# A fused two-block network on one core: the two opening slabs of each output projection worked in step, and seven eighths of one pair moved into a recurrence's last head

## The reference

```python
def gdn_mixer(h, w_in, conv_w, a_log, dt_bias, norm_g, w_out):
    ...
    o = chunk_gated_delta_rule(to_bhtd(q), to_bhtd(k), to_bhtd(v),
                               jnp.transpose(g, (0, 2, 1)), jnp.transpose(beta, (0, 2, 1)))
    o = jnp.transpose(o, (0, 2, 1, 3)).astype(h.dtype)
    o = rmsnorm(o, norm_g) * jax.nn.silu(gate.reshape(B, T, GDN_HEADS, GDN_HEAD_DIM))
    return o.reshape(B, T, GDN_VALUE_DIM) @ w_out

def swiglu(h, w_gate, w_up, w_down):
    return (jax.nn.silu(h @ w_gate) * (h @ w_up)) @ w_down

x = x + gate_m * y
x = x + gate_f * swiglu(h, ffn_w_gate[layer], ffn_w_up[layer], ffn_w_down[layer])
```

## Time and profile before

| what | value |
|---|---|
| time, median of 3 runs | 2578.01 us (2572.89, 2578.45, 2578.01) |
| the profiled execution's own time | 2574.89 us |
| its span, first to last instruction | 2573.1 us |
| mean granted clock of TensorE | 0.952 of full |
| TensorE matmul busy | 2323.3 us, 90% |
| TensorE weight load busy | 1831.7 us, 71% |
| GpSimd busy | 1204.3 us, 47% |
| VectorE busy | 1185.8 us, 46% |
| ScalarE busy | 609.6 us, 24% |
| DMA engines, mean busy share of the main queue | 30.1% |
| waits of GpSimd's L419 for TensorE's L459 | 539.3 us in 193 |

### The profile page before, as it was taken

One profiled execution on the slowest core, in us unless ns is written; L12 is line 12 of the kernel. 1 busy time (PEld: TensorE's weight loads), 2 busy tenths in 40 slices (PEclk: granted clock), 3 DMA queues, 4 the chain that ended last, 5 costly groups with the idle time before them and its releaser, 6 DMA issues.

```text
span 2573.1 us, 29814 instructions
## 1 busy us (share of the span) xinstructions
PE 2323.3 (90%) x12156; PEld 1831.7 (71%) x12156; DVE 1185.8 (46%) x1734; ACT 609.6 (24%) x1101; POOL 1204.3 (47%) x690
## 2 busy tenths in 40 slices
PE   4899998999999978889999997878898889989888
PEld 2677776778888755557888885556677767878766
DVE  5566666575454653225313136334452254554332
ACT  3243343131111232222202023332221121012112
POOL 1323222357777732115666665113446556656552
PEclk8999999899999989889999998889999999999989
DMA  6322222155555411002333332002223223323221
GB/s 212 98 86 67 80 76 65 57 165 172 189 164 191 136 64 35 25 25 77 104 98 94 96 93 80 25 25 67 72 73 92 81 82 107 97 83 98 83 82 58
DMA packets 361699, 236.23 MB, mean 92 GB/s; under 512 B 11126, under 2 KB 346204, under 8 KB 361436
## 3 DMA queue, kind: packets, MB, share of 16 engines
q1 hardware_dynamic: 360732, 230.40, 30.1%
q10 hardware_dynamic: 832, 3.93, 0.4%
HBM read 232.21 MB, written 2.10 MB: 91 GB/s over the span
## 4 chain that ended last, share of the span: by engine, by line
PE 82%; DVE 11%; ACT 3%; DMA 2%; issue 2%; POOL 1%; SPq 0%; DVEq 0%; ACTq 0%; POOLq 0%
PE bank L457 16%; PE bank L458 16%; PE bank L459 16%; PE bank L476 4%; PE bank L478 3%; PE bank L477 3%; PE bank L652 2%; PE bank L501 2%; DVE A L1774 2%; PE bank L971 1%; DMA WIDE<-in_ada_t 1%; PE bank L961 1%; DVE mx L1758 1%; PE bank L824 1%; PE bank L493 1%
## 5 line engine op out<-in xcount | busy, mean ns | idle before, releaser
L419 POOL TENSOR_SCALAR wH<-stage 128x1024 fp32r<-128x1024 f32 (+3 forms) x342 | 381.8, 1116 | 1312.7 <-PE bank L459 539.3
L421 POOL TENSOR_TENSOR wL<-stage,wH 128x1024 fp32r<-128x1024 f32 (+3 forms) x342 | 823.5, 2408 | 28.5
L457 PE MATMUL bank<-hH,wH 128*128 128x512 f32 x1108 | 439.9, 397 | 25.9 <-ACT A L1083 8.4
L458 PE MATMUL bank<-hL,wH 128*128 128x512 f32 x1108 | 435.8, 393 | 0.0
L459 PE MATMUL bank<-hH,wL 128*128 128x512 f32 x1108 | 435.3, 393 | 0.0
L457 PE MATMUL bank<-RA,wH 128*128 128x512 f32 (+1 forms) x900 | 327.5, 364 | 13.8 <-DVE A L1466 13.8
L458 PE MATMUL bank<-RA,wH 128*128 128x512 f32 (+1 forms) x900 | 325.8, 362 | 0.0
L459 PE MATMUL bank<-RA,wL 128*128 128x512 f32 (+1 forms) x900 | 325.8, 362 | 0.0
L457 PEld LDWEIGHTS bank<-hH,wH 128*128 128x128 f32 x1108 | 211.1, 191 | 76.1 <-issue 25.3
L459 PEld LDWEIGHTS bank<-hH,wL 128*128 128x128 f32 x1108 | 210.9, 190 | 44.6
L458 PEld LDWEIGHTS bank<-hL,wH 128*128 128x128 f32 x1108 | 211.2, 191 | 44.1 <-issue 0.7
(11 more groups left out here) (304 smaller groups left out, 3198.8 us busy)
## 6 DMA issues: line engine op xcount, KB each, us to landing
WIDE<-in_ada_t SPq DMA_DIRECT2D x48, 1024.0 KB, 5.9
stage<-in_ffn_w_gate SPq DMA_DIRECT2D x44, 512.0 KB, 3.8
stage<-in_ffn_w_up SPq DMA_DIRECT2D x44, 512.0 KB, 3.8
stage<-in_gdn_w_in SPq DMA_DIRECT2D x32, 512.0 KB, 4.1
stage<-in_ffn_w_down SPq DMA_DIRECT2D x32, 512.0 KB, 4.0
stage<-in_c_wkv SPq DMA_DIRECT2D x32, 512.0 KB, 3.8
stage<-in_o_w_in SPq DMA_DIRECT2D x32, 512.0 KB, 4.0
stage<-in_e_w_in SPq DMA_DIRECT2D x26, 512.0 KB, 3.8
```

The lines of the kernel that those rows point to most:

```text
L419: pool.tensor_scalar(high[:, 0:n], raw[:, 0:n], 1.0, 0.0, ALU.mult, ALU.add).then_inc(w_high, 1)
L421: pool.tensor_tensor(low[:, 0:n], raw[:, 0:n], high[:, 0:n].bitcast(F32), ALU.subtract).then_inc(w_split, 1)
L457: pe.matmul(bank[:, 0:n], h[:, k, c], xh[:, k, :], start=first and k == 0, stop=False)
L458: pe.matmul(bank[:, 0:n], h[:, k, c], xl[:, k, :], start=False, stop=False)
```

## The change

TensorE's program alone is changed. First, a residual begins with its slabs 0 and 1 in step: chunk 0 of slab 0, chunk 0 of slab 1, chunk 1 of slab 0, and so on, then the other six slabs as before. The transposes behind block 0 in `x1_out` come behind the pair. Second, in head 7 the fills are no longer empty: over the head they issue 14 of the 16 chunks of the opening pair of `gdn_out`, of blocks 0 to 6, at 14/32 of the pace of the other heads' fills; `gdn_out` itself begins with block 7.

```diff
-            def residual(name, xh, xl, kc, ready, count, r=None, behind=None):
+            def residual_chunk(name, xh, xl, kc, n, k, j):
 
                 s0, u0 = SLAB0[name], USE0[name]
-
-                def turn(i, first=False):
+                if n == 0:
+                    pe.wait_ge(w_split, s0 + j + 1)
+                    free(j, u0 // 2)
+                h, l = (w[:, k, :] for w in halves(s0 + j, kc))
+                pe.matmul(acc[j][:], h, xh[:, k, :], start=n == 0, stop=False)
+                pe.matmul(acc[j][:], h, xl[:, k, :], start=False, stop=False)
+                mm = pe.matmul(acc[j][:], l, xh[:, k, :], start=False, stop=n == kc - 1)
+                if n == kc - 1:
+                    mm.then_inc(slab_done, 1)
+
+            def residual(name, xh, xl, kc, ready, count, r=None, behind=None, order=None, begun=0):
+
+                s0, u0 = SLAB0[name], USE0[name]
+
+                for n in range(begun, kc):
+                    pe.wait_ge(ready, count - kc + n + 1)
                     for j in range(2):
-                        if first and j == 0:
-
-                            pe.wait_ge(w_split, s0 + 1)
-                            free(0, u0 // 2)
-                            for k in range(kc):
-                                pe.wait_ge(ready, count - kc + k + 1)
...
-                            mm.then_inc(slab_done, 1)
-                        else:
-                            slab(s0 + i * 2 + j, j, u0 // 2 + i, xh, xl, kc)
-                            if behind:
-                                behind(i * 2 + j - 1)
-
-                turn(0, True)
-                for i in range(1, KD // 2):
-                    turn(i)
+                        residual_chunk(name, xh, xl, kc, n, order[n] if order else n, j)
+                if behind:
+                    behind(0)
+                for i in range(2, KD):
+                    slab(s0 + i, i % 2, u0 // 2 + i // 2, xh, xl, kc)
+                    if behind:
+                        behind(i - 1)
                 if r is not None:
                     summed_squares(r)
...
-                def fill(*chunks):
+                def fill(first, end):
                     if ahead:
-                        head_sums(i + 1, range(*chunks))
+                        head_sums(i + 1, range(first, end))
+                    else:
+                        for c in range(14 * first // 32, 14 * end // 32):
+                            pe.wait_ge(y_ready, c // 2 + 1)
+                            residual_chunk("gdn_out", yH, yL, KD, c // 2, c // 2, c % 2)
...
-            residual("gdn_out", yH, yL, KD, y_ready, 8, 1)
+            residual("gdn_out", yH, yL, KD, y_ready, 8, 1, begun=KD - 1)
```

More of the change, by code:

```diff
@@ L538, in out_squares @@
                 mm.then_inc(ss_done, 2)
-            def residual(name, xh, xl, kc, ready, count, r=None, behind=None):
+            def residual_chunk(name, xh, xl, kc, n, k, j):
                 s0, u0 = SLAB0[name], USE0[name]
-                def turn(i, first=False):
-                    for j in range(2):
-                        if first and j == 0:
-                            pe.wait_ge(w_split, s0 + 1)
-                            free(0, u0 // 2)
-                            for k in range(kc):
-                                pe.wait_ge(ready, count - kc + k + 1)
[L552 to L555, removed]
-                            mm.then_inc(slab_done, 1)
-                        else:
-                            slab(s0 + i * 2 + j, j, u0 // 2 + i, xh, xl, kc)
-                            if behind:
-                                behind(i * 2 + j - 1)
-                turn(0, True)
-                for i in range(1, KD // 2):
-                    turn(i)
```

## The result

| | before | this change |
|---|---|---|
| time, median (all executions) | 2572.03 us (2566.62 to 2578.45, 10) | 2584.99 us (2573.97 to 2594.61, 10) |
| ratio, 95% interval | | 1.0047, 1.0026 to 1.0068 |
| profiled execution, its span | 2574.89, 2573.1 us | 2573.97, 2572.2 us |
| its mean granted clock of TensorE | 0.952 | 0.961 |

The change is **12 us slower** (0.0047 × 2572 = 12.1; interval 6.7 to 17.5). The profiled execution is the quickest of its ten, with the highest clock, so the two spans say nothing of the change. Two executions of kernels further down, 3040.55 and 3884.72 us at a granted clock of 0.731 and 0.555, are slow ones and are in no median or ratio.

The account below looks back on a forecast made before the run. TensorE holds 82% of the chain of waits, with almost no wait for interleaving to remove. Terms -1.5 + 5.0 + 1.8 + 1.8 + 3.2 + 1.3 = +11.6 on 2576.1 gave 2588 us, 8-in-10 range 2579 to 2598.

Parts of the forecast that it names:

- Head 7 and gdn_out: Fourteen chunks moved into head 7's fills gain 1.5 us instead of 9.5; bounds: loss 2.8, gain 5.4.
- gram: Head 7's first gram product, behind a chunk waiting for slab 1's split, starts at 446.3, 9.9 us late.
- the copy: Head 7's copy at L1606 comes at 452.7, 5.6 us late, as VectorE meets only the third split.
- the last y: Head 7's last y comes at 485.4; the last two chunks wait for it and run at the 1.2 GHz level.
- Nine closings: Slab 2 waits for bank 0 after each pair: 0.55 us each in nine plain residuals, +5.0 us.
- Four openings: After a feed-forward pair, slab 1's first chunk waits 0.45 us for bank 1, four times: +1.8 us.
- Part 0 of the first network: At its opening slab 1's split ends later than its first chunk wants it: +1.8 us.
- The last down projection: VectorE sets its end and starts late, making up a 0.63 us wait: +3.2 us, bounds +1.0 and +6.0.
- x1_out: TensorE turns block 0 over right behind the pair and waits for its update and copy: +1.3 us.
- banks that come back in time: Rival: updates release banks within the pair's 0.91 us, closings and x1_out vanish, head 7 fully relieved: 2573 us; chance 0.06.
- The head gets no relief: Rival: VectorE still meets splits, head clock stays low, last down projection costs 6: +18.7 us, 2595; chance 0.17.
- Half absorbed: Rival: better phase in the last down projection, closings 0.33 each, head 7 gives 4: +4.9 us, 2581; chance 0.12.

Follow-up runs that it names:

- the staggered kernel, Experiment 4: The change with slab 1 three chunks behind slab 0 in the eleven residuals other than gdn_out, against before: 2578.21 us, 1.0024.
- experiment 5: Slab 1 three chunks behind in ten residuals, last down projection as before, head 7 and gdn_out as changed; against before: 2577.31 us (1.0035), then 2572.41 us (0.9996).
- the second profile: The change timed and profiled once more without edit, against before: 2586.30 us, 1.0055.
- head only: Fourteen chunks in head 7 and gdn_out as in the change, the other eleven residuals as before; against before: 2568.88 us, 0.9991.
- experiment 6: Other residuals as before; against before: chunks only from fill 10, 2569.79 us; gdn_out's first two loads earlier with the change's fills, 2563.25 us; those loads alone, 2567.67 us.
- Experiment 3: Against before: only the last down projection in step, no chunks in head 7, 2578.59 us (1.0026); the change without that projection, 2584.88 us (1.005).

## Why the prediction was right

The forecast was 2588 us, +11.6 on the profiled execution. The places of the profile add up to 13.6, the timings give 12.1 and 14.1. Its base of 2576.1 came from four executions; over ten the median of before is 2572.03, and that rather than a term is why 2588 lies 3 us above the measured 2584.99. The single places are shown by the traces. Their sum is not confirmed to better than some 5 us: the interval of the change runs from 6.7 to 17.5, and three later timings came out above what their places give: the change without the last down projection by 4 us, the staggered kernel by 5, the first timing of experiment 5 by 10 (its second by none). Term by term:

- **Head 7 and gdn_out, -1.5: measured -1.5** (-2.3 in the second profile, -2.7 in head only). By its steps: gram 9.6 late (9.9 forecast), the copy 5.0 (5.6), the squares' product 2.5 and the last y 2.2, each counted on top of the 1.04 us. The hold at slab 1's split, the relief for VectorE and the unfilled wait for the last y all showed; experiment 6 tied the hold to the load. That the value is hit to 0.1 us is luck: the last y was 0.7 us less late than the forecast's 2.95, since VectorE met none of the splits where the third was forecast, and behind it 13 matmuls started at the 1.2 GHz pace (483.66 to 489.37) where six and 0.6 us were forecast. In head only it was six, and the gain 2.7.
- **Nine closings, +5.0: measured +5.0.** Distances of 0.64 to 0.75 us instead of 0.23 sum to 4.3 over the nine, and 0.08 at each restart gives 0.7. Experiment 4 takes them away by giving the bank back earlier. The weight load at 629.32 stands 0.03 us before its matmul, as in the earlier trace rows. The Trainium skill's rule of weight loads pulled ahead (TensorE: Matmul & The Clock Gate, Step-by-step: what each phase is for) holds no more for this wait than for that one.
- **Four openings, +1.8: measured +2.2** (0.65 to 0.77 us of distance, and the slow restart). **Part 0 of the first network, +1.8: measured +1.8** (618.50 - 616.58 - 0.23, and 0.11).
- **The last down projection, +3.2: measured +4.9, the mis-sized term.** The late start was right (+3.6 for 3.85). What failed is "VectorE finds blocks 0 and 1 both at hand and makes up the wait that it had between them": it did, but its 27 operations then took 29.9 us instead of 27.9, because the new phase against GpSimd's splits is a worse one. Experiment 3 shows the same without the rest of the change. The bounds had this possibility, the value didn't. The forecast also put nothing on the stretch behind, which gave back 0.8 of the 4.9. The Trainium skill (SBUF — State Buffer, Who interferes with whom) says that a VectorE instruction with two inputs in SBUF contends with a GpSimd one that reads SBUF; the rows agree: `hL` takes 0.80 us alone and up to 2.80 beside a split, the update, which reads one operand from a bank, keeps 0.74 us.
- **x1_out, +1.3: measured +1.2** (1.44 - 0.23). Later slabs of e_out, x0_out and o_out add nothing: VectorE catches up, as forecast.

Of the rivals, banks that come back in time needed an update ending 0.9 us after slab 0's last matmul, and TensorE waited for it at each. "The head gets no relief" fell with the 0.87 us of L1602, though its dearer tail was half right. "Half absorbed" was wrong in each part.

## What to carry over

Interleaving two accumulations left TensorE's pace as it was, 0.227 us a matmul, but it moves both banks' returns next to each other. Count the time from a bank's last write to its next use before and after, and stagger the pair by as much as the reader takes. Filling an idle stretch with other work pays more if that work's own inputs are there before the stretch begins (4.6 us against 2.7 for the same 14 chunks). Here, by the profiles, the order of two loads was worth as much as the 14 chunks. And where an engine sets a stage's end, shift its start only after looking at which of its operations will then run beside those of another engine that stretch them.

## What the runs showed of the hardware

One thing I had not counted on: how much executions of one kernel differ in the attention stretches, and how closely the mean granted clock tells it. Over 83 executions of before, from 2561.94 us at a clock of 0.959 to 2581.01 at 0.950, a line of 1.9 us per 0.001 of clock leaves a scatter of 1.6 us. A profile's span is therefore to be read with its clock. The line holds for before only: the sixteen executions of the change lie 19 us above it, where places and timings give 12 to 14, and why is open. Two kernels within 10 us of each other are compared by stretches that repeat, such as the feed-forward ones behind each network's first part (0.1 us), or by some twenty executions each: the first six of experiment 5 gave an interval wholly above 1, which the next twelve did not repeat.
